# Seven of eight head sums of the differential squares as two rounded matmuls, one tile later

## The reference, cut to what matters

```
def rms_normalize(x, eps=EPS):
    xf = x.astype(F32)
    return xf * lax.rsqrt(jnp.mean(xf * xf, axis=-1, keepdims=True) + eps)

def diff_attention(z, q_norm, k_norm, lq1, lk1, lq2, lk2, subln, lambda_init):
    ...
    q, k, v = jnp.split(z.astype(F32), 3, axis=-1)
    q = rms_normalize(q.reshape(B, S, H, 2, DIFF_QK)) * q_norm.astype(F32)
    k = rms_normalize(k.reshape(B, S, H, 2, DIFF_QK)) * k_norm.astype(F32)
    ...
```

## Time and profile before

| what | value |
|---|---|
| median of three executions | 1289.22 us (1288.03 to 1290.96) |
| the profiled execution, its own time | 1291.47 us |
| its span in the trace | 1289.70 us |
| PE busy | 1253.3 us, 97% |
| DVE busy | 699.2 us, 54% |
| ACT busy | 568.5 us, 44% |
| POOL busy | 530.7 us, 41% |
| mean granted clock of PE | 0.997 of full |

### The profile page before, as it was taken

The page is one execution under the profiler, slowest core; times in us unless marked ns, Lnnn a source line. Parts: engine busy times, 40 slices in busy tenths (PEclk is TensorE's granted clock), DMA queues, the critical chain, the costliest instruction groups (busy, mean ns, idle before and its releaser), DMA issues.

```text
span 1289.7 us, 20794 instructions
## 1 busy us (share of the span) xinstructions
PE 1253.3 (97%) x8570; PEld 1019.5 (79%) x8570; DVE 699.2 (54%) x1093; ACT 568.5 (44%) x870; POOL 530.7 (41%) x424
## 2 busy tenths in 40 slices
PE   6999999999999999999998899999999999999999
PEld 5788888866678888767786767788788888888999
DVE  3250004886431266686557657265565665766773
ACT  6541444786665233354544544353422221224452
POOL 6544454322234544534242126331444444546321
PEclk9999999999999999999999999999999999999999
DMA  9836795612115452412220013310222222224554
GB/s 387 348 131 243 248 230 191 163 50 97 51 66 188 122 163 79 181 66 76 69 107 16 3 66 131 135 61 34 99 98 98 81 87 94 99 88 172 166 185 151
DMA packets 24907, 165.05 MB, mean 128 GB/s; under 512 B 2792, under 2 KB 2920, under 8 KB 11504
## 3 DMA queue, kind: packets, MB, share of 16 engines
q1 hardware_dynamic: 20448, 128.15, 27.9%
q10 hardware_dynamic: 2064, 24.07, 5.0%
q0 software_dynamic: 2304, 11.54, 4.5%
HBM read 157.43 MB, written 29.38 MB: 145 GB/s over the span
## 4 chain that ended last, share of the span: by engine, by line
PE 89%; DVE 4%; ACT 3%; POOL 2%; issue 1%; DMA 0%; SPq 0%; DVEq 0%; ACTq 0%
PE banks L488 87%; PE banks L495 2%; DVE arena L1985 1%; POOL h_low L2557 1%; DVE arena L1982 1%; DVE arena L1987 1%; POOL weights_low L2557 1%; DMA arena<-in_mem 0%; ACT weights_high L1192 0%; ACT arena L1238 0%; ACT memory_high L1248 0%; ACT arena L1416 0%; ACT arena L1417 0%; ACT arena L1415 0%; DVE arena L1943 0%
## 5 line engine op out<-in xcount | busy, mean ns | idle before, releaser
L2499 POOL TENSOR_TENSOR weights_low<-weights,weights_high 128x512 fp32r<-128x512 f32 x324 | 433.2, 1367 | 580.5 <-ACT weights_high L1192 580.5
L488 PE MATMUL banks<-h_high_low,weights_high 128*128 128x512 f32 x880 | 358.2, 407 | 1.6 <-ACT arena L1443 1.6
L488 PE MATMUL banks<-h_low,weights_high 128*128 128x512 f32 x880 | 348.9, 397 | 0.0
L488 PE MATMUL banks<-h_high_low,weights_low 128*128 128x512 f32 x880 | 348.8, 396 | 0.0
L1192 ACT ACTIVATE weights_high<-weights 128x2048 fp32r<-128x2048 f32 (+2 forms) x90 | 156.3, 1737 | 243.1 <-PE banks L488 226.0
L488 PEld LDWEIGHTS banks<-h_high_low,weights_high 128*128 128x128 f32 x880 | 166.0, 189 | 46.0 <-issue 5.8
L488 PEld LDWEIGHTS banks<-h_low,weights_high 128*128 128x128 f32 x880 | 166.0, 189 | 41.8 <-issue 3.6
L488 PEld LDWEIGHTS banks<-h_high_low,weights_low 128*128 128x128 f32 x880 | 165.8, 188 | 40.4
L488 PE MATMUL banks<-arena 64*64 64x64 f32 (+6 forms) x1800 | 118.1, 263 | 4.1 <-issue 2.6
L488 PEld LDWEIGHTS banks<-arena 64*64 64x64 f32 (+3 forms) x1800 | 85.9, 148 | 29.9 <-issue 23.2
L1238 ACT ACTIVATE arena<-banks 128x256 f32<-128x256 f32 (+4 forms) x82 | 41.9, 519 | 53.4 <-PE banks L495 35.1
(11 more groups left out here) (360 smaller groups left out, 2371.9 us busy)
## 6 DMA issues: line engine op xcount, KB each, us to landing
weights<-in_stream SPq DMA_DIRECT2D x82, 1024.0 KB, 4.8
sums_kept<-in_down POOLq DMA_DIRECT2D x16, 704.0 KB, 12.8
arena<-in_ada SPq DMA_DIRECT2D x8, 1024.0 KB, 11.9
weights<-in_down SPq DMA_DIRECT2D x9, 704.0 KB, 4.1
weights<-sums_kept SPq DMA_DIRECT2D x9, 704.0 KB, 4.0
sums_kept<-in_down ACTq DMA_DIRECT2D x2, 2816.0 KB, 21.4
sums_kept<-sums_kept ACTq DMA_DIRECT2D x2, 2816.0 KB, 12.6
h<-sums_kept SPq DMA_DIRECT2D x7, 704.0 KB, 4.2
```

What stands on the lines that cost most here:

```text
L488: ins = nc.tensor.matmul(o, lhsT, rhs, start=start, stop=stop, skip_group_check=skip)
L2499: nc.gpsimd.tensor_tensor(lo_of(c)[:, cols], raw_of(c)[:, cols], hi_of(c)[:, cols].bitcast(F32), ALU.subtract).then_inc(sem("weights_split ...
```

## The change

Seven of the eight head sums (dn0 to dn6) become two fp32r matmuls that add up in one bank: the rounded squares times a rounded `blk`, and the low part of the squares times the same. dn7 stays as it was. For that

- ACT writes `blk_r`, a rounded copy of `blk`, once, before a chunk of weights; it takes the memory of the attention masks of the first block, which are no longer used;
- ACT computes each of the seven squares a second time, with a rounded output (`qk_hi`, in the memory of `forget_rows`);
- DVE subtracts the two (`square_low`, into `qk_lo`, in the memory of `sums`);
- PE waits for DVE's subtraction (`qk_low`) where it waited for ACT's square;
- the sums stand later on PE: dn0 and dn1 behind dq4, dn2 and dn3 behind dq5, dn4 and dn5 behind dq6, dn6 behind dq7;
- on DVE `decayed(1)` stands ahead of the first `dqk_scaled`, and not behind the second.

```diff
@@ -231,15 +232,17 @@
-        sums = sb("sums", 4, T)
+        sums, sums_r = sb_both("sums", 4, T)
...
-        masks = sb("masks", 3, P, kind=BF16)
-        nF_rows = sb("forget_rows", 2, T)
+        with nc.sbuf_tensor("masks", [P, 3 * P], BF16) as held:
+            pass
+        masks, blk_r = view(held[:, :], (3, P)), sb("blocks", 3 * P // 2, kind=F32R)[:, 0:P]
+        nF_rows, nF_rows_r = sb_both("forget_rows", 2, T)
...
-        qk_sq, qk_rinv = sq, [acc, rms]
+        qk_sq, qk_lo, qk_hi, qk_rinv = sq, sums_r[:, 0:2, :], nF_rows_r, [acc, rms]
@@ -791,8 +794,15 @@
+            pe.wait_ge(sem("blocks"), 1)
+
             def dq_sum(t):
-                block_sum("dn", t, qk_sq[:, t % 2, :], "qk_squares")
+                if t >= SPLIT_SUMS:
+                    return block_sum("dn", t, qk_sq[:, t % 2, :], "qk_squares")
+                pe.wait_ge(sem("qk_low"), t + 1)
+                o = M.take(pe, ("dn", t))
+                mm(o, blk_r, qk_hi[:, t % 2, :], True, False)
+                mm(o, blk_r, qk_lo[:, t % 2, :], False, True, M.filled)
@@ -818,13 +828,10 @@
-            dq_sum(0)
-            dq_sum(1)
             for t in range(4, 8):
                 project("dq", 1, KD, h, T, first=t)
-                if t == 4:
-                    dq_sum(2)
-                dq_sum(t - 1)
+                for n in range(2 * t - 8, min(2 * t - 6, SPLIT_SUMS)):
+                    dq_sum(n)
@@ -1518,6 +1525,7 @@
             act.dma_start(x2_kept, xres).then_inc(sem("x2_stored"), 16)
+            high(blk_r, blk, sem("blocks"))
             split_weights()
@@ -1577,6 +1585,8 @@
                 nc.scalar.activation(qk_sq[:, t % 2, :], dqk[:, t, :], ACT.Square).then_inc(sem("qk_squares"), 1)
+                if t < SPLIT_SUMS:
+                    nc.scalar.activation(qk_hi[:, t % 2, :], dqk[:, t, :], ACT.Square).then_inc(sem("qk_hi"), 1)
@@ -2162,6 +2172,11 @@
+            def square_low(t):
+                dve.wait_ge(sem("qk_squares"), t + 1)
+                dve.wait_ge(sem("qk_hi"), t + 1)
+                low(qk_lo[:, t % 2, :], qk_sq[:, t % 2, :], qk_hi[:, t % 2, :], sem("qk_low"))
@@ -2173,20 +2188,29 @@
             dq_out(3)
+            square_low(0)
             for j in range(2):
...
+            square_low(1)
             decayed(0)
             dq_out(4)
+            decayed(1)
             dqk_scaled(0)
+            square_low(2)
             dqk_scaled(1)
-            decayed(1)
+            square_low(3)
             dq_out(5)
             dqk_scaled(2)
+            square_low(4)
+            dqk_scaled(3)
+            square_low(5)
             dq_out(6)
-            dqk_scaled(3)
+            dqk_scaled(4)
+            square_low(6)
+            dqk_scaled(5)
             dq_out(7)
-            for t in range(4, 8):
+            for t in range(6, 8):
                 dqk_scaled(t)
```

More of the change, by code:

```diff
@@ L68 @@
 DOWN_RAW, DOWN_HI = 5, 4
+SPLIT_SUMS = 7
 GROUPS = ((0, 3), (3, 6), (6, 9), (9, 11))
```

## The result

The changed kernel takes 1291.21 us (median of 11 runs, 1288.77 to 1295.23), the kernel before 1288.28 us on the same chip (median of 11 runs, 1287.31 to 1290.96). The ratio is 1.0022, 95% interval 1.0011 to 1.0032: 2.8 us slower. Forecast were 1292.2 us and +3.0 us; the forecast stood on 1289.22 us for the kernel before, whose median here is 0.94 us lower.

A forecast was written before the change was run, and what follows sets the result against it. It took PE to bound the kernel. Waits of 3.84 us less 2.36 saved gave +1.5, the clock +1.5: +3.0 on 1291.47 is 1294.5, less 2.25 for the median 1292.2 us; range 1287.0 to 1295.0.

The forecast's parts named there:

- A sum of two fp32r matmuls takes 0.47 us and saves 0.39.: On PE, each split sum takes 0.47 us against 0.86 plain; six ahead of dq7's end save 2.36 us.
- Low part 1 and three of `decayed(0)` are slowed by POOL, four operations in all.: On DVE, while POOL splits a weight chunk from 608.51, such operations take about 1.6 us in place of 0.68.
- Low part 2 is done at 623.06.: On DVE, its queue reaches and finishes low part 2 at 623.06 us, while PE wants it at 620.12.
- PE waits 3.04 us, and 0.80 more ahead of dn3.: On PE behind dq5, waits for DVE's low parts 2 and 3, 3.84 us in all.
- The clock falls behind the wait and costs 1.5 us.: PE's granted clock drops to 0.50 after the wait, losing 1.5 us, between 1.0 and 2.0.
- The sum.: Whole kernel: +1.5 us to dq7's end plus 1.5 for the clock, +3.0 us in all.
- dn6's saving is hidden.: Behind dq7, the seventh cheaper sum saves nothing, because ACT paces what follows and PE already waits 0.6 us.
- Low parts 4 to 6 come in time, with a margin of 1.2 us.: On DVE, low part 5 is done at 629.3 while dq6 ends at 630.5, so PE has no further wait.
- A microsecond of the stage is one of the whole time: PE is 89% of the chain, so time saved or waits added on PE count in full.
- the clock stays: Rival: PE's waits come but its clock stays full; +1.5 us, 1290.7 us, chance 0.20.
- DVE in time: Rival: low part 2 is there by 620.1, so PE doesn't wait; -2.4 us, 1286.5 us, chance 0.15.
- A second wait: Rival: one of low parts 4 to 6 is late too, costing 1 to 2.5 us more; 1294.2 us, chance 0.10.

The follow-up runs named there:

- e5: The changed kernel with decayed(1) moved behind low part 3 and low parts 4 and 5 one place earlier on DVE; 0.9991 of the kernel before.
- e8: The changed kernel without POOL's split of one weight chunk, ACT writing a rounded copy instead; 1287.94 us in one run, stage 27.40 us.
- e3: The changed kernel with 11 and 3 extra rounded matmuls in PE's waits ahead of dn2 and dn3; 1.0024 of the kernel before.
- e7: A repeat of e3, the changed kernel with 11 and 3 extra matmuls in PE's two waits; 1.0023 of the kernel before.
- e2: The changed kernel's later places and DVE order, but with all eight sums plain fp32 and no low parts; 0.9991 of the kernel before.
- e1: The changed kernel with only decayed(1) moved back behind low part 3 on DVE; 0.9992 of the kernel before.
- the filled kernels: The changed kernel with extra matmuls put into PE's waits, as in e3 and e7; 1.0024 and 1.0023 of the kernel before.
- e10: The changed kernel with six extra full-width matmuls in PE's wait ahead of dn2 and none ahead of dn3; 1.0021 of the kernel before.
- e6: The changed kernel as it is, run again beside e7; 1292.88 us, 1.0019 of the kernel before.

## Why the prediction was right

Step by step, with times of the stage.

- *A sum of two fp32r matmuls takes 0.47 us and saves 0.39.* Right: e5 shows six times 0.39 to 0.02 us.
- *Low part 1 and three of `decayed(0)` are slowed by POOL, four operations in all.* Right, at 1.42 to 1.82 us from start to start, against 1.6. e8 shows that POOL is the cause.
- *Low part 2 is done at 623.06.* It was 622.78; the profiled execution was 0.21 us ahead at the bonus sums, which makes 622.99. All 13 us of DVE's work ahead of it were laid out to within 0.1 us.
- *PE waits 3.04 us, and 0.80 more ahead of dn3.* By the starts it was 2.90 and 0.80: 3.70 where 3.84 was forecast. The difference is DVE, 0.07 us earlier as above, the way from DVE to PE, 0.05 us and not 0.1 (for which the prediction has no row), and rounding.
- *The clock falls behind the wait and costs 1.5 us.* From the start of dn3 to the end of dq7 there are two tiles of 5.61, one sum of 0.47 and a pair of 0.94, 12.63 us at full clock. It took 638.20 - 624.10 = 14.10: 1.47 us lost. e3 and e7, with the same delay and a full clock, give 1.35. I had put this term's weight on one earlier wait, and that carried; that it came within 0.03 of the middle of 1.0 to 2.0 is luck.
- *The sum.* 3.70 + 1.47 - 2.36 = 2.81 us; the stage shows 2.86, the whole time 2.8, the forecast was 3.0.
- *dn6's saving is hidden.* Right. From the end of dq7 to the start of dv it is 6.57 us, and 6.72 before; but e2, whose dn6 is a plain sum, has 6.58 too. So these 0.15 us come with the new order, and nothing of dn6's 0.39 came through.
- *Low parts 4 to 6 come in time, with a margin of 1.2 us.* Right: low part 5 was done at 629.06, 629.27 with the 0.21 us, where 629.3 was forecast. In e3 and e7, which have the same waits and a full clock, it was done 1.22 and 1.20 us ahead of the end of dq6. The margin holds for a PE that waits; with PE on time and another order (e1) low part 5 was 0.29 us late.
- *A microsecond of the stage is one of the whole time* (PE is 89% of the chain). It fits the changed kernel, 2.86 and 2.8, but isn't shown beyond the noise: e5's 2.34 in the stage stand beside 1.2 in the whole, with an interval from 2.7 to -0.3, and the filled kernels miss it.

Of the rivals, "the clock stays" is what e3, e7 and e10 make of the stage (+1.5 there, +1.5 worked out), and "DVE in time" is what e8 and e5 make of it (-1.9 and -2.3, against -2.4 worked out). "A second wait" didn't come. As that rival has it, low part 6 was slow beside POOL's next chunk (1.37 us), but it was done at 636.20, 2.0 us ahead of the end of dq7. The three cases are told apart by the two things named, DVE's time up to low part 2 and the empty time of PE. What the clock costs is seen in the stage alone: the whole times of e3 and e7 don't show it.

## What to carry to other kernels

When a bound engine's work is cut into cheaper pieces that need an input from another engine, lay out that engine's queue instruction by instruction, with the price that each has beside its neighbours, up to the time at which the input is wanted: here four operations beside POOL cost 4 us and helped to turn a gain of 2.4 us in the stage into a loss of 2.9. Waits of PE of 2.9 and 0.8 us then had a second price behind them, of 1.4 us in this stage. Moving the late piece ahead of work that nobody waits for yet gave most of the gain back for one moved line (e1, 1.93 us) and all of it for three (e5, 2.34 us), in the stage; in the whole time neither can be told from the kernel before.

## What the hardware showed

- **DVE beside POOL.** An operation of DVE on two tensors of SBUF starts the next one 0.60 us later with POOL idle, and 1.42 to 1.82 us later while POOL subtracts (6.40 us for four, 1.60 each); e8 shows both prices for the same instruction. The Trainium skill ("SBUF — State Buffer", SBUF: two separate sides) says that a DVE operation with two SBUF inputs and a GpSimd operation that reads SBUF take a shared pair of ports for a whole instruction, and the other blocks. The trace agrees: the slowed operations of DVE keep nearly the pace of POOL's, as if they took turns. From 593.65 us POOL splits a chunk in 5.05 us, while DVE's three operations there each read a bank and take 0.69 us, and 1.28 for two: neither engine is slowed.
- **The clock.** It fell late: 1.00 in 620 to 622 with PE busy 0.09 of 2 us, and through dn2; 0.53 from 623.75 to 624.00, in the second wait; 0.50 in 624 to 627 with PE busy 2.90 of 3. In e6 it fell in the second wait, too (0.69 from 624.75 to 625.00, PE busy 0.00). About half a filling of the first wait, six matmuls, kept it at 1.00.
- **A narrow matmul is dear for what it does.** Eleven of 64 columns took 1.31 us at a granted clock of 1.00, 0.12 each, against 0.234 for 512 columns: half the time for an eighth of the columns. Each of the eleven comes with a weight load of its own in the trace (1.4 us busy for the eleven on PEld); whether the load sets this pace no run here shows.
